# Four quarters of the MLPs in seven block products each instead of eight (Strassen's scheme)

## What is computed

```python
for l in range(DEPTH_2):                      # two layers
    ...                                       # mixers, h = h + mix @ w_out[l]
    z = rms_norm_2(h, norm2_g[l])
    h = h + jnp.square(jax.nn.relu(z @ w_mlp1[l])) @ w_mlp2[l]    # 1024 -> 4096 -> 1024
return rms_norm_2(h, final_norm_g)
```

## Time and profile before

| | |
|---|---|
| time, median of 3 runs | 2558.69 us (2558.06 to 2562.41) |
| the profiled execution's own time | 2555.62 us |
| its span, first to last instruction | 2553.8 us |
| PE busy | 2494.5 us, 98% of the span |
| DVE, ACT, POOL busy | 1407.6, 1015.4, 257.0 us |
| mean granted PE clock | 0.992 of full speed |

### The profile page before, as it was taken

How to read it: one execution, slowest core, us unless ns; L and a number is a source line. 1 busy time by engine, 2 the same in 40 slices (tenths; PEclk the granted TensorE clock), 3 DMA queues, 4 the chain that set the end, 5 groups by cost and what they waited for, 6 DMA issues and landing times.

```text
span 2553.8 us, 45667 instructions
## 1 busy us (share of the span) xinstructions
PE 2494.5 (98%) x19566; PEld 2044.6 (80%) x19566; DVE 1407.6 (55%) x1949; ACT 1015.4 (40%) x1672; POOL 257.0 (10%) x218
## 2 busy tenths in 40 slices
PE   7999999999999999999999999999999999999999
PEld 5766787788988888788888876888888876888887
DVE  4454897556766554566643556562453455552542
ACT  4354765343334223333333347331233356321232
POOL 0300002233410000111111010100001010100001
PEclk9999999989999999999999999999999999999999
DMA  7211210000016664233333221332333221233332
GB/s 284 94 57 58 75 58 26 3 4 4 4 56 219 212 208 141 80 99 97 93 96 98 87 67 50 99 99 92 98 99 98 84 67 57 93 99 94 96 99 74
DMA packets 82761, 231.27 MB, mean 91 GB/s; under 512 B 7808, under 2 KB 26624, under 8 KB 82432
## 3 DMA queue, kind: packets, MB, share of 16 engines
q1 hardware_dynamic: 81696, 226.52, 27.5%
q10 hardware_dynamic: 864, 1.84, 0.2%
HBM read 217.84 MB, written 10.49 MB: 89 GB/s over the span
## 4 chain that ended last, share of the span: by engine, by line
PE 91%; DVE 4%; ACT 2%; issue 1%; DMA 1%; POOL 0%; SPq 0%; POOLq 0%; DVEq 0%; ACTq 0%
PE ps L318 62%; PE ps L2740 6%; PE ps L1663 4%; PE ps L328 3%; PE ps L810 2%; PE ps L1688 1%; PE ps L1669 1%; PE ps L1704 1%; PE ps L799 1%; PE ps L2794 1%; PE ps L2825 1%; PE ps L1934 1%; DVE row_max L840 1%; PE ps L825 1%; PE ps L1744 1%
## 5 line engine op out<-in xcount | busy, mean ns | idle before, releaser
L299 DVE TENSOR_TENSOR w_lo<-ring,w_hi 128x1024 fp32r<-128x1024 f32 (+1 forms) x339 | 416.7, 1229 | 781.0 <-ACT w_hi L291 780.9
L291 ACT CAST w_hi<-ring 128x1024 fp32r<-128x1024 f32 (+1 forms) x339 | 354.0, 1044 | 905.9 <-PE ps L318 807.2
L318 PE MATMUL ps<-u_hi,w_hi 128*128 128x512 f32 x864 | 338.4, 392 | 2.5 <-DVE u_lo L2550 2.5
L318 PE MATMUL ps<-u_lo,w_hi 128*128 128x512 f32 x864 | 337.2, 390 | 0.0
L318 PE MATMUL ps<-u_hi,w_lo 128*128 128x512 f32 x864 | 337.1, 390 | 0.0
L318 PE MATMUL ps<-mid_hi,w_hi 128*128 128x512 f32 x672 | 261.4, 389 | 0.0
L318 PE MATMUL ps<-mid_lo,w_hi 128*128 128x512 f32 x672 | 261.4, 389 | 0.0
L318 PE MATMUL ps<-mid_hi,w_lo 128*128 128x512 f32 x672 | 261.4, 389 | 0.0
L318 PEld LDWEIGHTS ps<-u_hi,w_hi 128*128 128x128 f32 x864 | 162.7, 188 | 38.2 <-issue 3.2
L318 PEld LDWEIGHTS ps<-u_lo,w_hi 128*128 128x128 f32 x864 | 162.9, 189 | 34.1 <-issue 0.5
L318 PEld LDWEIGHTS ps<-u_hi,w_lo 128*128 128x128 f32 x864 | 162.8, 188 | 33.7
(11 more groups left out here) (494 smaller groups left out, 4641.0 us busy)
## 6 DMA issues: line engine op xcount, KB each, us to landing
ring<-in_w_up SPq DMA_DIRECT2D x44, 512.0 KB, 3.6
ring<-in_w_in SPq DMA_DIRECT2D x42, 512.0 KB, 3.5
ring<-in_w_merge SPq DMA_DIRECT2D x32, 512.0 KB, 3.7
o_tok<-in_w_mod_rest SPq DMA_DIRECT2D x32, 512.0 KB, 5.1
ring<-in_w_mlp1a SPq DMA_DIRECT2D x32, 512.0 KB, 3.5
ring<-in_w_mlp2a SPq DMA_DIRECT2D x32, 512.0 KB, 3.5
ring<-in_w_mlp1b SPq DMA_DIRECT2D x32, 512.0 KB, 3.6
ring<-in_w_mlp2b SPq DMA_DIRECT2D x32, 512.0 KB, 3.6
```

What stands on the lines that cost most here:

```text
L291: nc.scalar.copy(w_hi[:, slot, 0:width], ring[:, n % RING, 0:width]).then_inc(*hi_ok.one())
L299: nc.vector.tensor_tensor(w_lo[:, slot, 0:width], ring[:, n % RING, 0:width], as_f32(w_hi[:, slot, 0:width]), ALU.subtract).then_inc(*lo_o ...
L318: mm = nc.tensor.matmul(dst[:, a:b], w[wi][:, k * P:(k + 1) * P], src[xi][:, k0 + k, a:b], start=start and k == wi == xi == 0, stop=stop a ...
```

## The change

In each layer, the first of the two halves of the MLP is made in two quarters of eight hidden tiles each, by a new function `stage_mlp_fast` that is called twice; four quarters in all. The second half of each layer stays as it was. A quarter has two stages.

The first stage makes eight hidden tiles from eight units, as before. They form the right operand of the projection as a 2 x 2 block matrix: tiles 0 to 3 and tiles 4 to 7 are the two rows of blocks, tokens 0 to 255 and 256 to 511 the two columns. The scheme needs sums of blocks: GpSimd makes one difference of 256 columns for each of tiles 0 to 3 and three for each of tiles 4 to 7. ACT and DVE make high and low parts of 2 blocks (tiles 0 to 3) and 5 blocks (tiles 4 to 7, in two parts of 512 and 768 columns). GpSimd also makes the four weight sums of the first pair of output tiles.

The second stage makes the projection to eight output tiles in four pairs. For each pair the two units are four blocks of 128 x 512; GpSimd makes four sums of them (512 columns each); seven operands (three blocks, four sums) are split by ACT and DVE into four half slots of `w_hi` and `w_lo`; PE makes seven products of 12 matmuls with 256 columns (before: four units of 24 matmuls with 512 columns for a pair); ACT copies one product to SBUF, DVE makes seven additions of 256 columns from PSUM and GpSimd four more in SBUF into `x`.

The core of the diff; parts left out are further waits' bookkeeping and the declaration of tiles:

```diff
-            for name in ("in2", "out2", "mlp1a", "mlp2a", "mlp1b", "mlp2b"):
-                add(f"{name}_{layer}")
+            add(f"in2_{layer}")
+            add(f"out2_{layer}")
+            for q in range(2):
+                units.extend(t_w[f"mlp1a_{layer}"][KD * q:KD * (q + 1)])
+                units.extend(t_w[f"mlp2a_{layer}"][q::2])
+            add(f"mlp1b_{layer}")
+            add(f"mlp2b_{layer}")
...
+            def fast_high(act, i):
+                p, j = divmod(i, 7)
+                if j in OF_RAW:
+                    landed(act, p, OF_RAW[j])
+                else:
+                    after(act, fast_pre, 16 * f + 4 * p + OF_SUM[j] + 1)
+                if i < 4:
+                    act.wait_ge(*slot_free(first - 2 + i // 2))
+                else:
+                    after(act, fast_done, 28 * f + i - 3)
+                nc.scalar.copy(half_slot(w_hi, i), source(i)).then_inc(*fast_hi.one())
+            def fast_low(dve, i):
+                after(dve, fast_hi, 28 * f + i + 1)
+                nc.vector.tensor_tensor(half_slot(w_lo, i), source(i), as_f32(half_slot(w_hi, i)),
+                                        ALU.subtract).then_inc(*fast_lo.one())
...
+                # first stage, GpSimd
+                    for n in range(KD):
+                        k = n % 4
+                        pool.wait_ge(*squared.at(n + 1))
+                        if n < 4:
+                            nc.gpsimd.tensor_tensor(g_f[:, k, 1, :], g_f[:, k, 2, :], g_f[:, k, 0, :],
+                                                    ALU.subtract).then_inc(*made_t.one())
+                            continue
+                        b = h_f[:, k % 2]
+                        nc.gpsimd.tensor_tensor(b[:, 2, :], b[:, 1, :], g_f[:, k, 1, :],
+                                                ALU.subtract).then_inc(*made_t.one())
+                        nc.gpsimd.tensor_tensor(b[:, 3, :], b[:, 1, :], g_f[:, k, 2, :],
+                                                ALU.subtract).then_inc(*made_t.one())
+                        pool.wait_ge(*made_t.at(4 + 3 * k + 1))
+                        nc.gpsimd.tensor_tensor(b[:, 4, :], b[:, 0, :], b[:, 2, :],
+                                                ALU.subtract).then_inc(*made_t.one())
+                        for which in ((S1,), (S2,), (S4, S3), ())[k]:
+                            weight_sum(pool, 0, which)
...
+                # first stage, ACT
+                    for n in range(KD):
+                        k = n % 4
+                        act.wait_ge(*unit_used.at(n + 1))
+                        split_hi(act, n + 2)
+                        for i in range(2 * (n - 6), 2 * (n - 5)) if n > 5 else ():
+                            fast_high(act, i)
+                        if n < 4:
+                            act.wait_ge(*made_t.at(n + 1))
+                            nc.scalar.copy(g[0][:, k], g_f[:, k, 0:2, :]).then_inc(*high.one())
+                        else:
+                            act.wait_ge(*squared.at(n + 1))
+                            nc.scalar.copy(h[0][:, k, 0:2, :], h_f[:, k % 2, 0:2, :]).then_inc(*high.one())
+                            act.wait_ge(*made_t.at(4 + 3 * (k + 1)))
+                            nc.scalar.copy(h[0][:, k, 2:5, :], h_f[:, k % 2, 2:5, :]).then_inc(*high.one())
...
+                # first stage, DVE
+                    for n in range(KD):
+                        split_lo(dve, n + 2)
+                        for i in range(2 * (n - 6), 2 * (n - 5)) if n > 5 else ():
+                            fast_low(dve, i)
+                        dve.wait_ge(*unit_used.at(n + 1))
+                        nc.vector.scalar_tensor_tensor(out=r[:, n % 2, :], in0=ps[:, n % 4, :], scalar=0.0,
+                                                       in1=rstd[:], op0=ALU.max,
+                                                       op1=ALU.mult).then_inc(*evac.one())
+                        dve.wait_ge(*evac.at(n + 1))
+                        nc.vector.tensor_tensor(dst, halves, halves, ALU.mult).then_inc(*squared.one())
+                        if n > 4:
+                            low_of_sums(k - 1)
+                        ...
+                    low_of_sums(3)
...
+            c1, c2 = slice(0, LAT // 2), slice(LAT // 2, LAT)
+            low_needed = {0: lambda k: -8, 1: lambda k: -8, 2: lambda k: 2 * k - 7, 3: lambda k: 2 * k - 7}
...
+                # second stage, GpSimd
+                    for p in range(4):
+                        if p < 3:
+                            weight_sum(pool, p + 1, S1)
+                            weight_sum(pool, p + 1, S2)
+                        after(pool, fast_x1, 4 * f + p + 1)
+                        add(x[:, 2 * p, c1], x1[:, p % 2, :], 28 * f + 7 * p + 3)
+                        add(x[:, 2 * p, c2], u2[:, p % 2, :], 28 * f + 7 * p + 5)
+                        if p < 3:
+                            weight_sum(pool, p + 1, S4)
+                            weight_sum(pool, p + 1, S3)
+                        add(x[:, 2 * p + 1, c2], u3[:, p % 2, :], 28 * f + 7 * p + 6)
+                        add(x[:, 2 * p + 1, c1], u3[:, p % 2, :], 28 * f + 7 * p + 7)
...
+                # second stage, PE
+                    for i in range(28):
+                        p, j = divmod(i, 7)
+                        w = half_slot(w_hi, i), half_slot(w_lo, i)
+                        moving = [t[:, :, j, :] for t in g] if j < 2 else [t[:, :, j - 2, :] for t in h]
+                        after(pe, fast_lo, 28 * f + i + 1)
+                        ...
+                        for k in range(4):
+                            if p == 0:
+                                pe.wait_ge(*low.at(low_needed[j](k) if j in low_needed else 0))
+                            for wi, xi in ((0, 0), (0, 1), (1, 0)):
+                                mm = nc.tensor.matmul(region(p, j), w[wi][:, k * P:(k + 1) * P], moving[xi][:, k, :],
+                                                      start=k == wi == xi == 0,
+                                                      stop=k == 3 and wi == 1)
+                        mm.then_inc(*fast_done.one())
...
+                # second stage, DVE, after product i: the additions from PSUM, then
+                        if i + 4 < 28:
+                            fast_low(dve, i + 4)
+                        elif i in (25, 27):
+                            split_lo(dve, KD + i // 27)
...
                 with ExitStack() as s2:
+                    tiles = fast_tiles(s2)
+                    stage_mlp_fast(u, x, rstd, tiles, sums_of_squares)
+                    stage_mlp_fast(u, x, rstd, tiles)
+                with ExitStack() as s2:
                     mid = split_pair(s2, "mid2", KF2 // 2, LAT)
-                    stage_mlp1(u, mid, KF2 // 2, rstd, sums_of_squares)
-                    stage_project(mid, x, KF2 // 2, sums=False)
                     stage_mlp1(u, mid, KF2 // 2, rstd)
```

More of the change, by code:

```diff
@@ L147, with __init__, count @@
 class Signal:
-    def __init__(self, sem):
-        self.sem, self.base, self.total = sem, 0, 0
+    def __init__(self, sem, before=0):
+        self.sem, self.base, self.total, self.before = sem, before, before, before
+    def count(self, n):
+        return self.sem, self.before + n
     def one(self):
@@ L255, in build, with later, fast_place, normal_number @@
                                               by_head + [part["gr"]], [])}
-            for name in ("in2", "out2", "mlp1a", "mlp2a", "mlp1b", "mlp2b"):
-                add(f"{name}_{layer}")
+            add(f"in2_{layer}")
[5 more added lines that the diff above has]
+            add(f"mlp2b_{layer}")
         loaded = [top.enter_context(nc.semaphore(f"unit_loaded{s}")) for s in range(RING)]
         unit_used, hi_ok, lo_ok = sig("unit_used"), sig("w_hi_made"), sig("w_lo_made")
-        at = {"issued": 0, "used": 0, "hi": 0, "lo": 0}
+        at = {"issued": 0, "used": 0, "hi": 0, "lo": 0, "fast": 0}
+        fast_at = []
+        def later(name, home):
+            if name not in signals:
+                signals[name] = Signal(signals[home].sem, signals[home].total)
+            return signals[name]
+        def fast_place(n):
+            for f, a in enumerate(fast_at):
+                if a <= n < a + KD:
+                    return f, n - a
+            return None
+        def normal_number(n):
+            return n + 1 - sum(min(max(n - a, 0), KD) for a in fast_at)
+        def ring_free(n):
+            if fast_place(n) is None:
+                return lo_ok.sem, normal_number(n)
+            f, i = fast_place(n)
+            return signals["fast_lo"].count(28 * f + 7 * (i // 2) + 6 + i % 2)
+        def slot_free(n):
+            if fast_place(n) is None:
+                return unit_used.sem, normal_number(n)
+            f, i = fast_place(n)
+            return signals["fast_done"].count(28 * f + (26 if i == KD - 2 else 28))
```

(13 more changed lines are left out.)

160 lines of the change are left out of this document (155 added, 5 removed).

## The result

The changed kernel took 2604.49 us (median of 4 runs, 2603.99 to 2617.49), the kernel before 2559.74 (4 runs, 2558.06 to 2562.41). The ratio is 1.0178 with a 95% interval of 1.0145 to 1.0211: 45 us slower, against a forecast of 2602.5 and a range of 2560 to 2630.

The account below looks back on a forecast made before the run. PE was taken as the bound, busy 98% of the span. Per quarter, 14.2 us lost (11.3 + 2.7 + 0.2) less 3.2 gained gave +11.0, +43.8 in four: 2602.5 us against 2558.7, range 2560 to 2630.

Parts of the forecast that it names:

- The gain: PE's products in a quarter: 40.3 us replace eight units of 43.5, gaining 3.2 a quarter, 12.8 in four.
- The prices and the exclusion: Operation times from the earlier trace; GpSimd and VectorE SBUF operations take turns, each holding memory its duration less 0.14 us.
- Rival B: GpSimd blocks less: product 2 waits 2.34 us, +3.0 us a quarter, 2570.5 us; chance 0.17.
- The timetable: Written-out order of all engines around T, the end of a quarter's first stage on PE; 11.3 us lost there.
- ACT's late turn: End of first stage: ACT starts its last tile work at T+6.24 instead of T+0.28, delaying product 2's weights.
- The step that failed: Start of second stage: products 0 and 1 run from T+0.28 to 3.16, needing only tiles 0 to 3.
- the list of added waits: Units only reordered; the added waits on `fast_x1` and `fast_post` are met by then.
- the three gaps: PE waits 5.48 us ahead of product 2, 2.83 ahead of its last quarter, 2.14 ahead of product 4.
- a later join: Product 4 needs tile 7's differences and its own weights' low part (16.43); 2.14 us lost.
- no such fall is taken in: PE's waits of some us in a quarter could lower the granted clock; the forecast left this out.
- The second stage: Low parts and GpSimd take 11.4 us per pair against PE's 10.1; six waits of 0.26 to 0.63, 2.7 in all.
- the timetable without exclusion: Rival B's written-out order: waits of 2.34, 2.31 and 1.51 us; 6.2 lost, +3.0 a quarter; chance 0.17.

Follow-up runs that it names:

- with GpSimd nearly free and the order mended: Changed kernel with GpSimd operations on 32 columns, PE's separate waits per product and ACT's later cast; 2563.22 us, ratio 1.0006 to the kernel before.
- the probe: Old kernel plus three unread GpSimd operations of 128 x 512 per hidden tile, two-input then one-input halves, beside MLP first projections; span 2555.2 us against 2553.8.
- the kernel with its own waits: Changed kernel with PE's single wait for the last ReLU replaced by each product's wait for its own PSUM bank; ratio 1.0155 to the kernel before.
- the kernel with GpSimd nearly free: Changed kernel with every GpSimd operation of the four quarters on 32 columns instead of 256 or 512; 2567.86 us, ratio 1.0038 to the kernel before.
- the pair with GpSimd nearly free: Changed kernel with GpSimd operations on 32 columns, without and with 30 unread matmuls filling PE's gap; ratios 1.0038 and 1.0019 to the kernel before.

## Why the prediction came out

**The gain.** 3.2 us a quarter was right: 0.1198 us for a matmul of 256 columns in the second stage wherever the clock was 1.00, as in the earlier trace rows. The best that was measured, with GpSimd nearly free and the order mended, kept 0.9 us of the 3.2.

**The prices and the exclusion.** Right. No run switches the exclusion off by itself in the changed kernel; but the probe shows it apart from the change, with the sizes of the earlier trace rows (2.33 for 1.23, against 2.10 there), and the PSUM operations free as the earlier trace rows said. Rival B, no exclusion, falls by that: product 2 would have waited 2.3 us, and in the kernel with its own waits it waited 4.2 to 5.3. "GPSIMD Engine Reference" in the Trainium skill, section Specifications, names contention with VectorE instructions of two SBUF inputs; the probe agrees for a two-input GpSimd operation (1.69 for 0.69 us), and the one-input operation held none (0.69).

**The timetable.** ACT's late turn at T+6.2 (6.0 measured), the last quarter of product 2 at T+12.6 (12.5, in the kernel with its own waits), product 4 at T+16.5 (16.4), the end at T+54.5 (55.1).

**The step that failed: "Products 0 and 1 need only tiles 0 to 3; their weights are ready at T+0.22, so they run from 0.28 to 3.16."** Their operands are ready, but PE's own program waits for the last ReLU ahead of all products. It is a wait of the change that the list of added waits left out. That ReLU ends at T+9.7 (forecast 9.8), so the three gaps forecast as 5.48, 2.83 and 2.14 were one of 9.6, and what the text gave as the mark of its being right (a gap of 5.5 ahead of the third product, 2.8 inside it) was not there. The sum held all the same. At the full clock PE would come to product 4 at T+9.7 + 4 x 1.44 = T+15.5, before its operands at T+16.5; with the fall of the clock it came at T+17.8 to 18.1. GpSimd's and DVE's timetable for the second stage doesn't depend on that, and the kernel with its own waits and the changed one end within 0.3 us of each other in every quarter. So two terms were left out, the wait and the clock, and a later join took both in. The prediction had the join but didn't argue from it; that these omissions cost nothing in the total was luck. In the kernel with GpSimd nearly free, where that join is gone, the omitted clock fall put the forecast 1.9 us a quarter too early.

**The clock.** Of PE's waits and the clock the prediction said that "no such fall is taken in". The fall came. After 9.6 us of waiting 24 matmuls ran 0.21 us apart in place of 0.12, 2.2 us. Filling the gap gave nothing back in the changed kernel (T+55.2 against 55.1), since PE then waited 0.7 us for product 4's weights and the rest, with the restarts, for those of the second stage. Where nothing follows that hides it, it costs 1.5 to 2.4 us a quarter, shown by the pair with GpSimd nearly free. The forecasts for the kernels with GpSimd nearly free and with the weight sums nearly free, made without it, came out 1.8 to 1.9 us too early a quarter.

**The second stage.** 2.7 us in six waits were forecast. Measured are three waits of 0.4 in the changed kernel with their restart, 2 us, and four behind product 5 in the one with its own waits (0.41 to 0.44 each). The size is near, and the cause as well: with the weight sums on 32 columns they vanish.

**The share of the causes,** in us a quarter from the ends above: order of ACT 2.1; the wait for all ReLUs 0 by itself; GpSimd's time 9.0 with the order as it is, of which weight sums 3.5. They overlap: with both, 55.1 falls to 42.6, by 12.5, not by 11.1. How much of GpSimd's 9.0 is its bare duration and how much exclusion stays open; the timetable without exclusion ended at T+46.5, which would make it 8.0 for exclusion, but no run shows that.

## What to carry to other kernels

An arithmetic saving on PE has to be set against the boundary where its new operands are made: here, in each quarter, 3.2 us of matmuls gained against 12 lost at the start of the second stage (9.7 of waiting, 2.2 of slow clock), because GpSimd, VectorE and ScalarE took 7.3 to 8.4 us for the operands of a tile that PE makes in 5.44. Before giving GpSimd work with two inputs beside a VectorE that subtracts in SBUF, count both engines' times as one resource, and look for every wait of PE's own program, not of the operands alone. When two runs with quite different waits end at the same time, find the later join that takes both in (here, by setting the start times of every engine beside each other), and test it by filling or moving one of the waits.

## What was not expected of the hardware

- A GpSimd operation with one input (`TENSOR_SCALAR`) held no VectorE operation in the probe, but was no faster there: 1.49 to 2.11 us for 128 x 512 beside a busy VectorE, with a median of 1.72, against 1.29 for two inputs alone. What it takes alone, no run shows.
- The granted clock fell to 0.50 behind PE's wait of 9.6 us and to 0.58 over the 4 us behind a wait of 4.1, and was 1.00 in the stretch that begins 5.2 us behind the longer one. 72 matmuls that nobody reads kept it at 1.00.
- The low part of a tile (0.69 us alone) took 1.69 beside two-input GpSimd operations, and the low part of a weight (1.23 alone) 2.33. The time that was added, 1.0 to 1.1 us, is most of one GpSimd operation of 1.29 and hardly depends on the held operation's own length; the square, which came later in such an operation, was held for 0.39.
